# Four score buffers, and the low parts of five weight pieces moved from GpSimd to VectorE, in a kernel of three mixer layers

## What is computed

```python
def dsa_mixer(h, w_in, w_out):
    proj = h @ w_in
    q, k, v, qi, ki, wi = jnp.split(proj, offs, axis=-1)
    q, k, qi, ki = (apply_rope(t, cos, sin) for t in (q, k, qi, ki))
    wi = wi * (IDX_HEADS ** -0.5 * IDX_DIM ** -0.5)
    def block(args):                       # 128 queries
        rel = jax.nn.relu(jnp.einsum('bthd,bsd->bths', qi_blk, ki))
        score = jnp.einsum('bths,bth->bts', rel, wi_blk)
        score = jnp.where(causal[None], score, -jnp.inf)
        _, idx = lax.top_k(score, k_sel)   # 64 keys of each query
        ...                                # softmax attention over these keys
    out = lax.map(block, (q_b, qi_b, wi_b, starts))
    return out @ w_out
```

## Time and profile before

| | us |
|---|---|
| three runs | 1359.85, 1361.86, 1361.92 |
| median | 1361.86 |
| the profiled execution | 1365.05 |
| its span in the trace | 1363.1 |

### The profile page before, as it was taken

How to read it: one execution, slowest core, us unless ns; L and a number is a source line. 1 busy time by engine, 2 the same in 40 slices (tenths; PEclk the granted TensorE clock), 3 DMA queues, 4 the chain that set the end, 5 groups by cost and what they waited for, 6 DMA issues and landing times.

```text
span 1363.1 us, 22148 instructions
## 1 busy us (share of the span) xinstructions
PE 1310.7 (96%) x8283; PEld 1138.6 (84%) x8310; DVE 903.8 (66%) x1441; ACT 667.4 (49%) x1119; POOL 415.9 (31%) x213
## 2 busy tenths in 40 slices
PE   6999999999889999999999999999999988999998
PEld 5877999988667799997888888799999957899998
DVE  6977333346975633334664766489999986699997
ACT  5755444444454544444264454355555533455553
POOL 3005444443201444444254321120000002344453
PEclk9999999998979999999899899999999999999999
DMA  7026666645203566663475522354445414266663
GB/s 224 16 92 202 186 185 186 188 129 185 94 31 98 164 187 186 187 195 97 138 223 151 176 90 75 93 151 143 141 139 156 135 62 131 79 190 194 193 186 108
DMA packets 166365, 197.15 MB, mean 145 GB/s; under 512 B 9981, under 2 KB 131325, under 8 KB 166269
## 3 DMA queue, kind: packets, MB, share of 16 engines
q1 hardware_dynamic: 164939, 191.54, 46.4%
q10 hardware_dynamic: 1362, 4.74, 1.1%
HBM read 195.20 MB, written 1.05 MB: 144 GB/s over the span
## 4 chain that ended last, share of the span: by engine, by line
PE 69%; DVE 22%; issue 4%; ACT 2%; DMA 1%; POOL 1%; DVEq 0%; SPq 0%; ACTq 0%
PE acc L625 21%; PE wk L571 11%; PE wk L573 11%; PE wk L572 11%; DVE LO L1830 4%; DVE arena L2357 2%; PE acc L604 2%; PE wk L1061 1%; PE acc L571 1%; PE acc L1087 1%; PE acc L572 1%; PE acc L573 1%; DVE LO L447 1%; DVE arena L1841 1%; DVE arena L2356 1%
## 5 line engine op out<-in xcount | busy, mean ns | idle before, releaser
L447 POOL TENSOR_TENSOR LO<-raw,HI 128x1024 fp32r<-128x1024 f32 (+1 forms) x160 | 382.4, 2395 | 864.3 <-ACT HI L1306 822.8
L1306 ACT ACTIVATE HI<-raw 128x1024 fp32r<-128x1024 f32 (+3 forms) x382 | 364.9, 996 | 161.5 <-PE acc L625 65.6
L571 PE MATMUL wk<-XH,HI 128*128 128x256 f32 x1296 | 369.8, 285 | 4.8 <-DVE XL L1863 3.7
L572 PE MATMUL wk<-XL,HI 128*128 128x256 f32 x1296 | 366.6, 283 | 0.0
L573 PE MATMUL wk<-XH,LO 128*128 128x256 f32 x1296 | 366.5, 283 | 0.0
L447 DVE TENSOR_TENSOR LO<-raw,HI 128x1024 fp32r<-128x1024 f32 (+1 forms) x160 | 197.4, 1237 | 158.2 <-ACT HI L1306 157.8
L571 PEld LDWEIGHTS wk<-XH,HI 128*128 128x128 f32 x1296 | 248.3, 192 | 9.9 <-issue 6.0
L572 PEld LDWEIGHTS wk<-XL,HI 128*128 128x128 f32 x1296 | 248.4, 192 | 2.0
L573 PEld LDWEIGHTS wk<-XH,LO 128*128 128x128 f32 x1296 | 248.4, 192 | 0.0
L625 PE MATMUL acc<-HI,HH 128*128 128x512 f32 x424 | 131.9, 392 | 3.8 <-DVE HL L2400 3.1
L625 PE MATMUL acc<-LO,HH 128*128 128x512 f32 x424 | 131.1, 390 | 0.0
(11 more groups left out here) (361 smaller groups left out, 1942.1 us busy)
## 6 DMA issues: line engine op xcount, KB each, us to landing
raw<-in_mlp_w SPq DMA_DIRECT2D x128, 512.0 KB, 4.3
raw<-in_w_in SPq DMA_DIRECT2D x100, 512.0 KB, 4.2
raw<-in_w_up SPq DMA_DIRECT2D x44, 512.0 KB, 4.0
raw<-in_w_down SPq DMA_DIRECT2D x44, 256.0 KB, 3.2
raw<-in_att_w_in SPq DMA_DIRECT2D x16, 512.0 KB, 4.5
raw<-in_w_ssd_proj SPq DMA_DIRECT2D x16, 512.0 KB, 3.7
raw<-in_att_w_out SPq DMA_DIRECT2D x8, 512.0 KB, 4.3
raw<-in_w_out SPq DMA_DIRECT2D x8, 512.0 KB, 4.1
```

Of the source, the lines that this page charges most:

```text
L447: tensor_tensor(LO[:, s, cs], raw[:, s % 2, "ab".index(part), 0:m], HI[:, s, cs].bitcast(F32), ALU.subtract).then_inc(S(f"lo_{part}"), 1)
L571: mm(o, lh, rh, start=start, stop=False, skip_group_check=skip)
L572: mm(o, lh, rl, start=False, stop=False, skip_group_check=skip)
L1306: A(HI[:, s, j * m:(j + 1) * m], raw[:, s % 2, j, 0:m], ACT.Copy).then_inc(S(f"hi_{part}"), 1)
```

## The change

`rel` gets four buffers, and ScalarE waits for `rel_used` only in jobs 4 and 5, for jobs 0 and 1. GpSimd stops after half b of piece 41, waits until VectorE has written half b of piece 46 (`lo_b` at 47) and goes on with piece 47. VectorE writes both halves of pieces 42 to 46: 42 and 43 where their a halves were, 44 ahead of the rotation of the keys rather than behind it, 45 behind that rotation and ahead of the first index block (before: behind that block), 46 behind `rotate_queries(0)` (before: ahead of it). Its half a of piece 47 goes from behind the second index block into turn 2 of the attention loop. On ScalarE the high part of piece 46 goes from between `index_relu(3)` and `index_relu(4)` to behind `tile_evac(4)`, and that of piece 49 from turn 1 of the loop to turn 6.

```diff
-        rel = carve(8592, 2, 512)
+        rel = [carve(at, 512) for at in (8592, 9104, 3072, 3584)]
...
+            upto(P_ATT + 4)
+            while ring.n <= P_ATT + 9:
+                ring.next()
+            pool.wait_ge(S("lo_b"), P_ATT + 10)
             upto(P_ATT + 14)
...
-                if job >= 2:
-                    act.wait_ge(S("rel_used"), job - 1)
+                if job >= 4:
+                    act.wait_ge(S("rel_used"), job - 3)
...
-                if n == 1:
+                if n == 6:
                     hi_to(P_ATT + 12)
...
-            lo_to(P_ATT + 6)
+            dve.wait_ge(S("lo_b"), P_ATT + 5)
+            lo_both()
+            lo_both()
...
+            lo_both()
             rotate_keys()
-            lo_to(P_ATT + 7)
+            lo_both()
...
-                    lo_to(P_ATT + 9)
                     rotate_queries(0)
-            lo_to(P_ATT + 10)
+                    lo_both()
...
-                if n in (N1 - 2, N1 - 1):
+                if n in (2, N1 - 2, N1 - 1):
                     lo_next()
```

More of the change, by code:

```diff
@@ L1513, in index_relu @@
                 act.wait_ge(S("rel_psum"), job + 1)
-                if job >= 2:
-                    act.wait_ge(S("rel_used"), job - 1)
-                A(rel[:, job % 2, :], accf[:, 1024 + (job % 2) * 512:1536 + (job % 2) * 512], ACT.Relu)\
+                if job >= 4:
+                    act.wait_ge(S("rel_used"), job - 3)
+                A(rel[job % 4], accf[:, 1024 + (job % 2) * 512:1536 + (job % 2) * 512], ACT.Relu)\
                     .then_inc(S("rel_read"), 1)
@@ L1530, in _ @@
             index_relu(3)
-            hi_to(P_ATT + 9)
             index_relu(4)
@@ L2164, in _ @@
                         hd = h0 + 2 * b
-                        r = rel[:, job % 2, b * K:(b + 1) * K]
+                        r = rel[job % 4][:, b * K:(b + 1) * K]
                         w = wi_s[:, tb, hd:hd + 1]
```

## The result

The changed kernel is slower: 1369.74 us median of 20 runs against 1362.32 of 20 runs of the kernel before. The ratio is 1.0053, with a 95% interval from 1.0034 to 1.0072, so +7.2 us, between 4.6 and 9.8. The prediction was +5.4, with a range from 1361.5 to 1371.0. The profiled execution has a span of 1367.9 us (before 1363.1, in an execution of 1365.05 us that lay 2.7 above the median).

What follows compares the result with a forecast made beforehand. VectorE's chain was taken to bound the changed stretch, with TensorE's idle time free. Terms of 4.4 us up to the first masked scores and 1.0 at job 8 gave +5.4, from 1361.86 to 1367.3 us; range 1361.5 to 1371.0.

Steps and rivals of the forecast that it cites:

- VectorE's chain decides: From the keys' rotation to job 1's transposes only VectorE's time counts; TensorE losing 4.3 us of waits gains nothing.
- 42, 43, 44 ahead of the rotation: Six halves on VectorE before the keys' rotation: cost nothing; cover some 0.2 us thin, up to 0.3 if high part late.
- 45 ahead of the block, +3.7: Before the first index block VectorE idles 2.5 us for ScalarE's high part 45, then writes both halves: +3.7 us.
- the stall there, -2.0: In the first index block, without GpSimd beside it, the addition of 2.36 us becomes 0.36: -2.0 us.
- The two stalls in the second block, +2.0 and +1.9: GpSimd's 47b, then 48b, each hold VectorE's additions in the second index block: +2.0 and +1.9 us.
- 47a out of the block, -1.2: Half 47a leaves the second index block for VectorE's wait in loop turn 2, where it costs nothing: -1.2 us.
- 46 behind the rotation, 0: Around the first queries' rotation, 45a and 46a go and 46a and 46b come back, 2.36 us each: 0.
- Together 4.4 us at the first masked scores: Terms up to `largest1(0)`, 3.7 - 2.0 - 1.2 + 2.0 + 1.9: it and all following on VectorE start 4.4 us late.
- Job 8, +1.0: GpSimd's 49b holds job 8's multiplication: +1.0 us; 0 if it slips past, 1.4 if the small operation ahead is held too.
- The clock: TensorE's half-clock stretch: no term in the sum; edge shifts kept within the main case's own range, 1365.6 to 1369.0.
- the main case: Whole kernel: all terms hold, +5.4 us, median 1367.3; chance 0.40.
- the rival with the longer half clock: TensorE's longer wait keeps the clock low for another 6.82 us stretch: +3.4 us more, 1370.7; chance 0.11.

Runs made afterwards that it cites:

- e10_bufgate: Kernel before with four score buffers, and GpSimd waiting for the last index addition before 47b: ratio 1.0001.
- e2_45late: Changed kernel with both low halves of piece 45 behind the first index block, ahead of the first queries' rotation: ratio 1.0013.
- e1_gate6: Changed kernel with GpSimd also waiting for VectorE's last index addition before it writes 47b: ratio 0.9981.
- e8_loop: Changed kernel with low half 47a back behind the second index block and the high part of 49 back in turn 1: ratio 1.0046.
- e11_gate49: e9_next with GpSimd also waiting for VectorE's multiplication of job 8 before 49b: median 1357.80 us, ratio 0.9956.
- e3_hi49: Changed kernel with only the high part of piece 49 back in turn 1 of the attention loop: ratio 1.0105.
- e4_buffers: Kernel before with four buffers for the rectified scores and nothing else: ratio 1.0038.
- e5_busy: Changed kernel with 38 dummy matmuls ahead of job 2's scores and 18 ahead of job 3's on TensorE: ratio 1.0014.
- e9_next: Kernel before with four buffers, 42-44 on VectorE, 47a and high 49 late, high 46 earlier, GpSimd's halves held for searches, dummies in three TensorE waits: ratio 0.9972.

## Why the prediction was right

*VectorE's chain decides.* Right. TensorE's two waits went and 8.81 us came in their place, and e10_bufgate shows the four buffers at no gain when GpSimd is kept in its place.

*42, 43, 44 ahead of the rotation.* Right: the rotation's second half started straight behind the first, 0.15 us after the last matmul of TensorE's piece 41, where before the distance was 0.10. The cover was too thin by that 0.05.

*45 ahead of the block, +3.7, and the stall there, -2.0.* The block starts 3.75 us later behind the rotation (4.93 less 1.18), and its search 1.75 later, so both terms held. e2_45late corrects what lies behind the first: 1.4 us are 45's own.

*The two stalls in the second block, +2.0 and +1.9.* Measured 1.97 (5.58 less 3.61) and 2.08 (2.37 less 0.29). The second fell on the causal mask's addition and not on one of the seven. I had 48b starting 25.6 to 26.6 us behind the rotation (369.4 to 370.4), and it started at 26.75, with the seven over at 27.1; that one more operation with two SBUF inputs stood behind them, which I hadn't named, was luck. e1_gate6 shows GpSimd's halves as the cause.

*47a out of the block, -1.2.* Right: with it back, e8_loop has mask 0 at 39.2 instead of 38.0. *46 behind the rotation, 0.* Right: the second block starts 1.75 us late, just as the first search.

*Together 4.4 us at the first masked scores.* Measured 4.6.

*Job 8, +1.0.* Measured 1.2, within the bounds, but on another operation: the small tensor-scalar operation of line 2201, which belongs to job 9 and stands ahead of job 8's multiplication, took 1.36 us instead of 0.17, and the multiplication that I had named ran its 0.69. The bound of 1.4 had this operation held as well as the multiplication, not instead of it. e11_gate49 and e8_loop give the term as 1.1.

*The clock.* I took it as neutral with bounds. In the two traces it is nearly so. TensorE was at half clock for 23.9 us after (375.8 to 399.7), the first 4.9 of them inside its long wait, where they cost nothing, and for 17.0 us before (371.5 to 378.3 and 388.6 to 398.8). From mask 0 to the end it takes 69.2 us against 68.8, with 1.2 of job 8 in it, so the clock gave 0.8 back. That TensorE would wait longer and not be at full clock for jobs 1 to 4 was right.

*The sum.* +5.4 predicted, +5.0 between the two traces on the ruler, +7.2 (4.6 to 9.8) between the medians. The intervals agree, but the measured time lies between the main case and the rival with the longer half clock (1370.7), and the clocks of the executions bear on that. The traced execution of the kernel before had a mean granted clock of 0.983, lower than its usual one: the median of its 107 executions in the later comparisons is 0.987. The changed kernel's median is 0.984, that of its trace. At one and the same clock it is some 3 to 5 us longer: at 0.986 three executions of 1365.4 to 1366.6 stand against twelve with a median of 1362.7, at 0.984 four of 1369.0 to 1370.0 against one of 1365.1 (at 0.987 its only one, 1363.2, is 1.0 above the median of 48). The rest goes with the lower clock. The long wait goes with it too: the four kernels in which TensorE waits over 8 us ahead of job 2's scores (the changed one, e3_hi49, e4_buffers, e8_loop) have median clocks of 0.981 to 0.984, those with 2.7 to 7.4 us 0.986 to 0.987, and those with dummies there 0.989 to 0.991. So neutral on the clock was too kind by about 2 us, and it was the range that took it in. That the wait is the cause of the lower clock is argued from this order and from e5_busy; in which stretch the untraced executions lost it no run shows.

The Trainium skill's rule that I had weighed (SBUF - State Buffer, "SBUF: two separate sides": an exclusive lock, the first keeps it for its whole instruction) agrees with the holds of 2 us on operations with two SBUF inputs. A part of it that the prediction had not used may bear on two more: it counts operations of VectorE in a two-port mode among those that the lock holds, and it was tensor-scalar operations with one SBUF input that took 1.36 and 1.64 us. The traces show these two held; that it is that mode which holds them no run here shows.

## What to carry to other kernels

A low-priority engine that shares something with the one on the critical path should be told when to run, not only what: here one wait for a semaphore that was already there moved 4.8 us of GpSimd work from additions into a search and gave back 4 us. Whoever frees an engine of a wait should ask which transfers and which other engines that wait had been holding, since the four buffers alone cost 4.0 us in that way. And where an engine has to idle, its next work may run at half clock, so a gain that only lengthens its wait isn't neutral.

## What was not expected of the hardware

VectorE's MAX8, match-replace and reduce operations ran at their usual length beside GpSimd (0.43 and 0.41 us under 47b and 48b in e1_gate6, 0.69 under 49b in the changed kernel), but a tensor-scalar operation on two numbers per partition was held for 1.2 us (1.36 instead of 0.17), and one of 128 numbers for 1.4 (1.64 instead of 0.23). TensorE's clock fell to half inside a wait of 2.09 us in e5_busy, though 8.38 us of dummy matmuls at full clock had run shortly before; with all three waits partly filled it fell behind one of 1.94 us in e9_next and stayed at 1.0 through one of 1.93 us in e11_gate49.
